# The last tile of the embedding's projection is moved from the routing into the first expert pass

## The reference, cut to what matters

```
x = layer_norm(DN_ALPHA * x + mix)                       # x after the mixer
ffn = hier_moe(x, w_group, w_router, w_gate, w_up, w_down)
x = layer_norm(DN_ALPHA * x + ffn)
ple = sigmoid(x @ w_ple_gate) * (p @ w_ple_proj)         # p: the per-layer embedding, 256 wide
x = x + rms_norm(ple)

# hier_moe: best of 4 groups, then 2 of its 8 experts for each row; each row's result is
#   sum over its 2 experts e of gate_e * ((silu(row @ w_gate[e]) * (row @ w_up[e])) @ w_down[e])
```

## Time and profile before

| | |
|---|---|
| median of three runs | 975.97 us |
| the profiled execution | 975.77 us |
| its span, first to last instruction | 974.0 us |
| mean granted TensorE clock | 0.987 |
| busy: TensorE, VectorE, ScalarE, POOL | 96%, 44%, 25%, 10% |
| mean DMA rate | 254 GB/s |

### The profile page before, as it was taken

One profiled execution on the slowest core, in us unless ns is written; L12 is line 12 of the kernel. 1 busy time (PEld: TensorE's weight loads), 2 busy tenths in 40 slices (PEclk: granted clock), 3 DMA queues, 4 the chain that ended last, 5 costly groups with the idle time before them and its releaser, 6 DMA issues.

```text
span 974.0 us, 13892 instructions
## 1 busy us (share of the span) xinstructions
PE 934.2 (96%) x5256; PEld 558.0 (57%) x5256; DVE 427.5 (44%) x981; ACT 246.8 (25%) x531; POOL 96.8 (10%) x146
## 2 busy tenths in 40 slices
PE   9999999999999999999999999989999898998797
PEld 7777777777777766655678644443333333333343
DVE  0211467877634238687631244682111211113874
ACT  1122221132144115665730000131111111012244
POOL 0011211211212100000000000011211111010000
PEclk9999999999999989999999999999999999999899
DMA  9866888997897711111114991448999999998501
GB/s 374 335 246 230 290 301 308 325 342 277 283 354 252 256 44 47 31 36 41 66 47 155 369 422 76 169 145 356 420 422 425 425 420 424 422 406 320 211 22 65
DMA packets 63689, 247.38 MB, mean 254 GB/s; under 512 B 11109, under 2 KB 12014, under 8 KB 54118
## 3 DMA queue, kind: packets, MB, share of 16 engines
q1 hardware_dynamic: 45014, 191.29, 50.5%
q0 software_dynamic: 13216, 35.28, 9.8%
q10 hardware_dynamic: 5392, 19.93, 5.5%
HBM read 240.85 MB, written 18.05 MB: 266 GB/s over the span
## 4 chain that ended last, share of the span: by engine, by line
PE 78%; DMA 12%; DVE 6%; issue 2%; ACT 2%; SPq 0%; DVEq 0%; ACTq 0%
PE ps L892 21%; DMA arena<-in_wexp 10%; PE ps L1357 8%; PE ps L1281 6%; PE ps L1482 4%; PE ps L1377 4%; PE ps L1210 4%; PE ps L980 3%; PE ps L951 3%; PE ps L1065 3%; PE ps L883 3%; PE ps L1089 2%; PE ps L1029 2%; PE ps L1046 1%; PE ps L955 1%
## 5 line engine op out<-in xcount | busy, mean ns | idle before, releaser
L892 PE MATMUL ps<-arena 128*128 128x260 f32 x928 | 216.8, 390 | 0.4 <-DMA arena<-in_w 0.4
L892 PEld LDWEIGHTS ps<-arena 128*128 128x128 f32 x928 | 174.9, 192 | 35.7 <-issue 8.8
L1357 PE MATMUL ps<-arena 128*64 128x512 f32 x576 | 129.0, 601 | 11.4 <-DMA arena<-in_wexp 9.8
L1357 PEld LDWEIGHTS ps<-arena 128*64 128x64 f32 x576 | 42.1, 138 | 85.7 <-issue 83.2
L1857 DVE SCALAR_TENSOR_TENSOR arena<-arena,vec 128x512 f32<-128x512 f32 x120 | 81.7, 745 | 0.0
L2538 POOL DMA_DIRECT2D arena<-in_kv x96 | 51.7, 539 | 265.6 <-issue 259.5
L1377 PE MATMUL ps<-arena 128*64 128x512 f32 x288 | 65.8, 598 | 3.3 <-DMA arena<-in_wexp 3.3
L2364 DVE TENSOR_TENSOR arena<-ps,arena 128x256 f32<-128x256 f32 x18 | 7.6, 425 | 128.8 <-ACT arena L1715 128.8
L1281 PE MATMUL ps<-arena 128*128 128x512 f32 x128 | 58.4, 602 | 0.0
L1210 PE MATMUL ps<-arena 128*128 128x260 f32 x224 | 49.3, 383 | 0.0
L1210 PEld LDWEIGHTS ps<-arena 128*128 128x128 f32 x224 | 42.7, 190 | 6.4
(11 more groups left out here) (356 smaller groups left out, 1162.8 us busy)
## 6 DMA issues: line engine op xcount, KB each, us to landing
arena<-in_wexp SPq DMA_DIRECT2D x30, 2048.0 KB, 25.0
arena<-in_kv SPq DMA_DIRECT2D x160, 272.0 KB, 9.2
arena<-in_wexp SPq DMA_DIRECT2D x36, 1024.0 KB, 26.5
arena<-in_kv POOLq DMA_DIRECT2D x96, 272.0 KB, 7.4
arena<-in_w ACTq DMA_DIRECT2D x35, 512.0 KB, 7.2
arena<-in_wo SPq DMA_DIRECT2D x8, 512.0 KB, 3.7
arena<-in_w_out SPq DMA_DIRECT2D x4, 1024.0 KB
x_scratch<-arena SPq DMA_DIRECT2D x8, 512.0 KB, 3.6
```

Source lines behind the costliest of these rows:

```text
L892: y = mm(ps[:, b + h, 0:TH], w[:, k], xT[:, k, h * TH:(h + 1) * TH], start=(k == 0), stop=(k == KD - 1))
L1357: y = mm(ps[64 * x:64 * x + 64, 2, :], xgT[:, k, 64 * x:64 * x + 64], wx[slot][:, x, k * 512:(k + 1) * 512], start=(k == 0), stop=(k == KD ...
```

## The change

On TensorE ple_rows(4) leaves its place behind L1334 and stands in pass 0, behind gate_up(0), rows_in(1) and the gates' transpose, ahead of turn_h(0). The wait for s_ppe at 5 moves from ahead of pass 0 into down(0). The tile's banks become 6 and 7, by the table PLE_BANK, which leaves the banks of the other tiles as they were. On ScalarE ple_out(4) moves from ahead of rows_in(0) to behind gate(0) and rows_in(1).

```
+PLE_BANK = [2, 0, 2, 0, 6]
             def ple_rows(u, halves=(0, 1)):
-                t, b = ORDER[u], 2 - 2 * (u % 2)
+                t, b = ORDER[u], PLE_BANK[u]
@@ TensorE
             y.then_inc(s_rp, 1)
-            ple_rows(TILES - 1)
@@ down
                 if not (isinstance(p, int) and p == 0):
                     pe.wait_ge(m.ya, p)
                     pe.wait_ge(m.yd, p)
+                else:
+                    pe.wait_ge(s_ppe, TILES)
@@ TensorE, the passes
             rows_in(0, 0, 16)
-            pe.wait_ge(s_ppe, TILES)
@@
                 if p > 0:
                     slot, n = weight_slot(PASS[p - 1][1])
                     down(p - 1, slot, 32 * n)
+                else:
+
+                    ple_rows(TILES - 1)
                 turn_h(p)
@@ ScalarE
             def ple_out(u):
-                t, b = ORDER[u], 2 - 2 * (u % 2)
+                t, b = ORDER[u], PLE_BANK[u]
@@
-            for u in range(1, TILES):
+            for u in range(1, TILES - 1):
                 ple_out(u)
@@
                 gate(p)
                 if p + 1 < NPASS:
                     rows_in(p + 1)
+                if p == 0:
+                    ple_out(TILES - 1)
                 if p > 0:
```

## The result

The changed kernel takes 978.57 us (median of 20 runs, 977.44 to 981.45) against 975.52 us before, a ratio of 1.0033 with a 95% interval of 1.0024 to 1.0042. Measured again beside one more copy of the kernel before, it was 979.73 us against 975.41 us, 1.0040 (1.0026 to 1.0054). It is slower by 3 to 4 us; both medians are within 0.5% of the kernel before, and 979.0 was forecast.

What follows compares the result with a forecast made beforehand. The prediction took the passes to be bound by the expert weights' transfers. Load 4's data come 2.7 to 3.5 us late, taken as 3.1: 975.77 + 3.1 = 978.9, put at 979.0 for the median; range 974.2 to 983.0.

Steps and rivals of the forecast that it cites:

- rows_in(0) 0.8 us earlier: End of the routing: without the tile, rows_in(0) starts near 652.5 instead of 653.33, limited by the gather landing at 652.4.
- The transposes at half clock, 2.1 us: In rows_in(0): the eight large transposes, paced by their weight loads, take 2.1 us at half clock against 1.04.
- gate_up(0) at 8.5 us: First gate and up product in pass 0: starts at half clock, costing 1.4 us more than 7.09.
- the bound of 664.5: Latest time forecast for m.h to reach 1, after the first gate and up product; 664.2 expected, 662.51 before.
- m.h from 1 to 2 in 11.9 us: Pass 0, between the first and second gate and up products: the tile adds net 3.0 us to 8.94.
- Two holes on the queue, of 1.3 and 1.8 us: Weights' queue stands still ahead of load 3 until 665.6, and ahead of load 4 from 676.0 to 677.8.
- TensorE's lateness by itself costs nothing: In the passes: TensorE's waits for weights cover its lateness, so it adds 0 us.
- The new wait in down(0) costs nothing: Wait for s_ppe in down(0): ScalarE's copy of 1.02 us runs beside gate_up(1), so it adds 0 us.
- The tail behind the last weights is unchanged: After 878: the tail keeps its length; a changed length would show the forecast wrong.
- (2): Rival: load 4's hole closes through full clock in gate_up(0) and uncounted work; 0.9 us or nothing left, 976 to 977; chance 0.22.
- (1): Rival: clock stays low longer in gate_up(0) and the projection behind it; up to 984.6, slower by over 0.5%; chance 0.12.
- (3): Rival: clock doesn't fall, rows_in(0) and the whole queue start 0.8 us earlier at full clock; 975.0; chance 0.06.

Runs made afterwards that it cites:

- e6_split: Changed kernel with the tile's first 512 columns computed in the routing, the other 512 in pass 1, ScalarE copying both there; 977.24 us against 974.96 before.
- e1_both: Changed kernel with the tile computed once more, unused, in its old place in the routing, the real one staying in pass 0; 975.84 us against 975.16 before.
- e3_both_pass1: Changed kernel with an unused copy of the tile in the routing and the real one in pass 1; 973.90 us against 975.16 before, repeated 975.32 against 975.41.
- e2_pass1: Changed kernel with the tile and ScalarE's copy one pass later, behind gate_up(1) and ahead of down(0); 977.45 us against 975.16 before.
- e7_copy_late: Kernel before with the tile whole in the routing, in banks 3 and 7; only ScalarE's copy and its wait move as in the change; 973.98 us against 975.54.
- e4_twice0: Changed kernel with the tile computed twice in pass 0, into the same banks; 982.21 us against 975.16 before.

## Why the prediction was right

The forecast was 3.1 us, the runs gave 3.0 and 4.3. The mechanism held: the clock lost in the routing and the tile in pass 0 each opened a hole on the queue. That the first median meets the forecast this closely is partly luck, since a term that was too small, a landing less late than the queue's lag and a tail that was to stay as it was offset one another. By its steps:

- rows_in(0) 0.8 us earlier: 4.20 against 4.89 us from the list, 0.7. The gather landed and TensorE started at once. But the gain exists only against the first trace of before, in which the clock was low under the tile. In the second trace the tile takes 3.70 us, and the transposes start 4.17 us behind the list with the tile still in the routing; there, taking it away gains nothing:

```profile
649.78 1.06 PE L1346 MATMUL ps<-con,arena 128*128 128x128 f32 x8 [0.81 <-DVE pages L2330]
```

- The transposes at half clock, 2.1 us: 1.94. The bound of the row of weight loads was nearer, the other end, about 1 us, was wrong. That the transposes are paced by their loads, the reason given for it, isn't shown: in the changed kernel the eight loads are busy for 1.57 of the 1.94 us.
- gate_up(0) at 8.5 us: 9.40 and 8.94 in the two traces, with the clock at 0.50 for 4.6 us of it in the first. This term was too small by 0.5 to 0.9 us, and the bound of 664.5 (which is 16.1 from the list) was passed by 0.4: m.h came at 16.4 (15.9 in the second trace). What failed was the choice of rows: there the clock came back after 2.7 and 3.0 us of the products at half clock, here after 4.6. (The 2.7 us are an estimate, twice the 1.37 us that the product at 830.27 took longer.) The rule of the Trainium skill (TensorE: Matmul & The Clock Gate, PE-mode transpose), that transposes don't count as work for the clock as matmuls do, agrees with these traces, but they don't test it: eight transposes of 128 columns ran just ahead, and gate_up(0) began at half clock in all six; but the 2.88 us of matmuls in the routing of e6_split left the clock low as well.
- m.h from 1 to 2 in 11.9 us: 11.81. The tile took 3.44 us, 3.5 was forecast, and the 0.48 us of idle time went.
- Two holes on the queue, of 1.3 and 1.8 us: 1.7 and 1.8 by the rates. The lag of the queue was 3.7 and 3.3 us, the last weights landed 2.8 us later (3.1 forecast; 2.5 in the second trace). From 60 to 220 us behind the list both kernels move 423 GB/s in both traces, so the queue made nothing up there, as was argued from the DMA share of 1.01. The landing is all the same 0.8 to 0.9 us less late than the lag says; where the last 10 us make that up isn't shown.
- TensorE's lateness by itself costs nothing: the square of e1 to e3 shows it.
- The new wait in down(0) costs nothing: right in pass 0, 1.16 us in pass 1 (e2). ScalarE's earlier place was to give 0.04 us at most; the wait ahead of gate_up(0) is 1.05 us in both traces of before and 0.90 in every other, 0.15 less.
- The tail behind the last weights is unchanged: this failed, and a tail of another length was one of the forecast's own signs of being wrong. It is 95.94 and 96.19 us in the traces of before, 97.53 and 98.93 in those after. Two rows account for it to within 0.3 us. One, in both traces after, is the product that follows the last weights, 3.65 us before and 5.35 after; the other, in the second trace after alone, is the product of L1487 (L1482 before) behind a wait of some 5 us, 10.18 us where before has 8.62 and 8.90. In this order, before, changed, changed again:

```profile
878.19 3.65 PE L1377 MATMUL ps<-arena 128*64 128x512 f32 x16 [2.06 <-DMA arena<-in_wexp]
878.10 5.35 PE L1380 MATMUL ps<-arena 128*64 128x512 f32 x16 [2.11 <-DMA arena<-in_wexp]
909.62 10.18 PE L1487 MATMUL ps<-arena 128*128 128x512 f32 x16
```

The product of 5.35 us had the clock at 0.50 for some 3.4 us of it, behind a wait of 2.1 us, which is as long as in the kernel before (2.06), where the clock stood. That it comes from the change isn't shown: e7_copy_late, whose passes are those of before, has 5.35 us too, and e2_pass1 hasn't. Nor is it ruled out: all four traces with the tile in pass 0 have it (changed twice, e1_both, e4_twice0), and of the eight others only e7_copy_late. It adds 1.7 us to those executions that meet it, and with it the 2.8 and 2.5 us of the landing come to 4.2 to 4.5, above the first median's 3.0 and about the second's 4.3. How often it occurs in the executions without a profile stays open.

A reading that nothing rests on: the forecast gives the stretch ahead of the passes 76 and 169 GB/s; these are slices 25 and 26, and slice 27, in which the routing ends, has 145.

The rivals: (2), with a hole that closes, is refuted by the rows at 662 and 674. (1), the whole of gate_up(0) at half clock, was not reached, but it was nearer than the two rows made it look. (3) needed a clock of 1.00 at the transposes; it was 0.50.

Open: where the queue's lead of 1.3 to 1.6 us in e3_both_pass1 and its repetition comes from. gate_up(0) starts 0.2 to 0.9 us earlier there than in the two traces of before, which explains that much of it, the 0.15 us of the shorter wait included. e7_copy_late, which has the same place for ScalarE's copy, leads by 0.6 us. In all ten traces with the late copy the last weights land 0.3 to 1.0 us earlier than the lag at 60 us says, in the two of before within 0.3 us of it; why is open too.

## What to carry to other kernels

Where transfers set the time, ask of a moved block not whether TensorE has room for it, but which releases stand behind it in TensorE's order, and whether the queue runs dry before they come. A block of matmuls that "only fills a wait" may be what holds the clock up for the work behind it; taking it out can cost more than it frees, as here. And a queue that is full to the end keeps every early hole, so the first microseconds of such a stage are worth as much as any.

## What the runs showed of the hardware

Eight transposes of 128 x 128 in float32 take 1.04 us at full and 1.94 us at half clock. The same gate and up product takes 7.09 us at full clock and 8.57 to 9.40 us where it begins at half clock, behind the transposes and 1.7 to 4.5 us without work ahead of them. A wait of 2.0 to 2.3 us ahead of the down product that follows the last weights (the last but one of the kernel) left the clock up in seven traces and down in five, with the same instructions around it: whether a short pause costs anything isn't decided by its length alone.
